# A hybrid decoder step on one core: the projection in two token halves with the mLSTM between its pieces, decode attention alone

## The reference

```python
h = rmsnorm(x, pre_g)
u = h @ w_in                                # 1024 -> 3584 = 28 tiles of 128
qa, ka, va, za, xb, ob, zb = split(u)       # 4 tiles each
a = diff_attention(qa, ka, va)              # 4 heads; sample: 2048 cached keys in 16 pages of 128
a = headwise_rmsnorm(a) * silu(za)
xc = causal_conv(xb); xch = silu(xc)        # 4 taps
qb, kb, vb = xch @ wq, xch @ wk, xb @ wv    # per head, 4 heads of 128
gates = concat(qb, kb, vb) @ w_if + b_if    # input gate, forget gate
hb, C, n, m = mlstm_scan(qb, kb, vb, gates) # running state C (128 x 128 a head)
hb = headwise_rmsnorm(hb * sigmoid(ob)) + skip * xch
y = concat(a, hb * silu(zb)) @ w_out
x = x + rmsnorm(y)
x = x + rmsnorm(sigmoid(x @ ple_gate) * (p @ ple_w))
```

## Time and profile before

| | us |
|---|---|
| median of 3 runs | 1188.6 (1186.11 to 1190.7) |
| profiled execution, its own time | 1184.3 |
| its span, first to last instruction | 1182.6 |
| PE busy | 1007.3 (85%) |
| DVE, ACT, POOL busy | 480.1, 371.6, 72.6 |
| DMA moved | 126.3 MB |

### The profile page before, as it was taken

The page is one execution under the profiler, slowest core; times in us unless marked ns, Lnnn a source line. Parts: engine busy times, 40 slices in busy tenths (PEclk is TensorE's granted clock), DMA queues, the critical chain, the costliest instruction groups (busy, mean ns, idle before and its releaser), DMA issues.

```text
span 1182.6 us, 20550 instructions
## 1 busy us (share of the span) xinstructions
PE 1007.3 (85%) x7424; PEld 829.9 (70%) x7424; DVE 480.1 (41%) x1156; ACT 371.6 (31%) x845; POOL 72.6 (6%) x174
## 2 busy tenths in 40 slices
PE   4899999999995768878887778567788799989997
PEld 4899999999994656556566655344556688667773
DVE  5411010101104845555455455337886534352222
ACT  4322121222212043323323333236665432241111
POOL 2100000000002011001001001001110000000000
PEclk9999999999995689999999999769999899989998
DMA  6111121111103154765665665566000222212220
GB/s 200 41 54 48 43 56 36 54 38 52 54 1 107 35 185 143 226 193 186 210 205 186 207 208 188 171 239 274 2 1 1 76 72 92 73 45 81 81 82 26
DMA packets 88701, 126.32 MB, mean 107 GB/s; under 512 B 8744, under 2 KB 44713, under 8 KB 88636
## 3 DMA queue, kind: packets, MB, share of 16 engines
q1 hardware_dynamic: 88636, 125.44, 32.7%
HBM read 110.00 MB, written 15.41 MB: 106 GB/s over the span
## 4 chain that ended last, share of the span: by engine, by line
PE 65%; DVE 10%; SPq 7%; issue 6%; DMA 5%; ACT 4%; POOL 1%; ACTq 0%; DVEq 0%; POOLq 0%
PE ps L1433 30%; PE ps L1416 9%; PE ps L1417 9%; PE ps L1418 9%; PE ps L1436 8%; SPq L357 4%; SPq L362 3%; DVE pp L1282 3%; DVE pp L1295 2%; DMA Vr<-in_cache_v 2%; DMA Kr<-in_cache_k 1%; DMA Cs<-in_state_C 1%; DMA U<-in_x_prompt 1%; POOL si L561 1%; DVE Caug L1234 1%
## 5 line engine op out<-in xcount | busy, mean ns | idle before, releaser
L1416 PE MATMUL ps<-hhi,whi 128*128 128x352 f32 x672 | 218.6, 325 | 3.5 <-ACT U L588 1.8
L1417 PE MATMUL ps<-hlo,whi 128*128 128x352 f32 x672 | 216.8, 323 | 0.0
L1418 PE MATMUL ps<-hhi,wlo 128*128 128x352 f32 x672 | 216.5, 322 | 0.0
L878 DVE TENSOR_TENSOR wlo<-wst,whi 128x1024 fp32r<-128x1024 f32 x28 | 34.3, 1224 | 255.6 <-ACT whi L583 255.6
L1416 PEld LDWEIGHTS ps<-hhi,whi 128*128 128x128 f32 x672 | 127.2, 189 | 3.8 <-issue 3.8
L1417 PEld LDWEIGHTS ps<-hlo,whi 128*128 128x128 f32 x672 | 127.4, 190 | 0.0
L1418 PEld LDWEIGHTS ps<-hhi,wlo 128*128 128x128 f32 x672 | 127.1, 189 | 0.0
L588 ACT ACTIVATE U<-ps 128x352 f32<-128x352 f32 x84 | 38.7, 465 | 242.8 <-PE ps L1418 241.9
L1436 PE MATMUL ps<-ident,Kr 128*128 128x128 f32 x512 | 69.9, 281 | 37.4 <-DVE kTs L1114 22.0
L1433 PE MATMUL ps<-wh,rh 128*128 128x512 f32 (+1 forms) x288 | 93.2, 405 | 4.6 <-DVE wout_lo L1349 4.6
L1436 PEld LDWEIGHTS ps<-ident,Kr 128*128 128x128 f32 x512 | 58.1, 144 | 51.4 <-issue 37.5
(11 more groups left out here) (293 smaller groups left out, 1507.8 us busy)
## 6 DMA issues: line engine op xcount, KB each, us to landing
Kr<-in_cache_k SPq DMA_DIRECT2D x128, 256.0 KB, 2.7
Vr<-in_cache_v SPq DMA_DIRECT2D x128, 256.0 KB, 3.4
wst<-in_w_in SPq DMA_DIRECT2D x28, 512.0 KB, 3.8
out_y_prompt<-rows SPq DMA_DIRECT2D x16, 512.0 KB, 2.9
U<-in_x_prompt SPq DMA_DIRECT2D x8, 512.0 KB, 3.6
wout<-in_w_out SPq DMA_DIRECT2D x1, 4096.0 KB, 13.9
rows<-in_x_prompt SPq DMA_DIRECT2D x8, 512.0 KB, 4.7
wgate<-in_ple_gate_w SPq DMA_DIRECT2D x1, 4096.0 KB, 25.8
```

The source lines that it names most:

```text
L1416: nc.tensor.matmul(out, hi, hhi[:, k, cols], start=k == 0, stop=False)
L1417: nc.tensor.matmul(out, hi, hlo[:, k, cols], start=False, stop=False)
L1418: last = nc.tensor.matmul(out, lo, hhi[:, k, cols], start=False, stop=k == KC - 1)
```

## The change

What it does:

1. `U` is cut in two, `U0` (tokens 0 to 511 and the 32 sample tokens, 544 columns) and `U1` (tokens 512 to 1023). The order of weight tiles is xb, ob, zb, qa, ka, va, za. For the first half each weight tile is used in two pieces of 272 columns. Then all 28 weight tiles are loaded and split again, for the second half, each in two pieces of 512 columns by 4 of the 8 blocks of the contraction, both into the same bank. That makes 112 pieces.
2. The order of the head tiles is 0, 1, 2, 3, sample, 4, 5, 6, 7.
3. All pieces are stored with Copy. `gate_tiles` applies Sigmoid or Silu later, in place, on four tiles at once, six passes in all, with a load of the function table before and after.
4. The sample mLSTM runs after piece 10, with one to six pieces (`fill`) between its steps. The prompt mLSTM (`chunk(i)`) follows: chunks 0 to 3 between pieces of the first half's end and the second half's begin, chunks 4 to 7 after the conv of the second half. `FILLS` says how many pieces stand between the steps of a chunk. Each half has its own buffers. POOL no longer copies ob into `kbT`; PE transposes it straight from `U`.
5. Decode is alone, nine rounds written out on PE, ACT and DVE. K has a ring of 16 pages (all of a sequence), V of 8. Transposed keys (`kTs`) and scores have two buffers. The values of the previous sequence come in the second half of a round, two groups at a time.
6. SP: `numbers` and `pages` are as before. K of sequence 0 is loaded after the last piece, then 16 stores (states and sample rows) are issued, then the other rounds.

Core of the diff:

```diff
+HALF = SEQ // 2
+FIRST = HALF + SMP
+PIECE = FIRST // 2
+ORDER = [first + n for first in (XB, OB, ZB, QA, KA, VA, ZA) for n in range(4)]
...
+WEIGHTS_DONE = [2 * w + 2 if w < NT else NT + w + 1 for w in range(WEIGHTS)]
...
+FILLS = [(1, 0, 2, 1, 1, 1, 1)] + 3 * [(1, 1, 2, 1, 1, 1, 1)] + [(1, 0, 3, 3, 2, 2, 2), (1, 1, 3, 1, 1, 1, 2),
+                                                               (1, 1, 3, 1, 1, 1, 2), (1, 1, 3, 1, 1, 2, 2)]
```

On SP:

```diff
                 for g in range(GROUPS):
                     k_nums = None if last else numbers(i, g)
                     v_nums = None if first else numbers(i - 1, g)
                     if not last:
-                        if not (first and g < 4):
-                            sp.wait_ge(s["k_used"], i * GROUPS + (g - 3))
-                        pages(ck, Kr, GP * g % 8, k_nums, k_in[g % 4])
+                        if not first:
+                            sp.wait_ge(s["k_used"], i * GROUPS + (g - GROUPS + 1))
+                        pages(ck, Kr, GP * g, k_nums, k_in[g])
                     if not first:
-                        if not (isinstance(i, int) and i == 1 and g < 2):
-                            sp.wait_ge(s["v_used"], (i - 1) * GROUPS + (g - 1))
-                        pages(cv, Vr, GP * g % 4, v_nums, v_in[g % 2])
+                        if not (isinstance(i, int) and i == 1 and g < 4):
+                            sp.wait_ge(s["v_used"], (i - 1) * GROUPS + (g - 3))
+                        pages(cv, Vr, GP * g % 8, v_nums, v_in[g % 4])
...
+            sp.wait_ge(s["piece_done"], EVENTS)
+            stream_pages(0, True, False)
+            sp.wait_ge(s["C_done"], CH)
+            put("out_state", io["C_prompt"][0, 0].rearrange("h d e -> d h e"), Caug[:, :, 0:DH])
...
             stream_pages(1, False, False)
```

On ACT (`fill` stands on each engine, with that engine's share of a piece):

```diff
+            def gate_tiles(tile, hf, fn):
+                U = (U0, U1)[hf]
...
+                nc.scalar.activation(U[:, tile:tile + 4, :], U[:, tile:tile + 4, :], fn).then_inc(s["gated"], 1)
...
+            def fill(n=1):
+                for p in range(filled[0], filled[0] + n):
+                    if p < 2 * NT:
+                        if p:
+                            evict(p - 1)
+                    elif p % 2 == 0:
+                        evict(2 * NT + p // 2 - NT - 1)
+                    if p % 2 == 0 and p // 2 + 1 < WEIGHTS:
+                        split(p // 2 + 1)
...
             act.wait_ge(*done["nT_ready"])
             act.wait_ge(s["cs_in"], 32)
             copy(Cs[:, :, DH], ps[:, 5, 0:SMP], "n_stored")
...
+            fill(4)
```

On PE a chunk goes: projections, `fill(before_turn)`, `finish(i - 1)`, `fill(before_gates)`, gates with the turned k and v and q x k, `fill(before_rows)`, rows and mask products, `fill(before_inter)`, q x state, `fill(before_intra)`, weights x v and the state update, `fill(before_turn_ob)`, ob turned, `fill(after)`. A piece and a decode round are:

```diff
+            def piece(p):
+                w, part = p // 2, p % 2
...
+                pe.wait_ge(s["wlo_ready"], w + 1)
...
+                if e >= 4 and not (p >= 2 * NT and part):
+                    pe.wait_ge(s["u_stored"], e - 3)
...
+                for k in ks:
+                    w_hi, w_lo = whi[:, w % 2, k, :], wlo[:, w % 3, k, :]
+                    mm(out, w_hi, hi[:, k, cols], k == 0, False)
+                    mm(out, w_hi, lo[:, k, cols], False, False)
+                    last = mm(out, w_lo, hi[:, k, cols], False, k == KC - 1)
...
+                def values(g):
+                    pe.wait_ge(v_in[g % 4], 32 * (2 * (i - 1) + g // 4 + 1))
...
+                    last.then_inc(s["v_used"], 1)
...
+                for g in range(GROUPS):
+                    if i < NSEQ:
+                        keys(g)
+                    if g == 1 and i >= 1:
+                        turn_weights()
+                    if i < NSEQ and g >= 1:
                         scores(g - 1)
...
+                    if i >= 1 and g >= 4:
+                        values(2 * g - 8)
+                        values(2 * g - 7)
```

More of the change, by code:

```diff
@@ new lines, in rtok @@
+        def rtok(tile, t0, n):
+            if t0 >= SEQ:
+                return r0[:, tile, HALF + t0 - SEQ:HALF + t0 - SEQ + n]
+            return r0[:, tile, t0:t0 + n] if t0 < HALF else r1[:, tile, t0 - HALF:t0 - HALF + n]
+        rows = [place(f"rows{n}", [P, D], offset=u0_base + VA * FIRST * 4 + n * D * 4) for n in range(2)]
+        rows.append(place("rows2", [P, D], offset=u1_base + VA * HALF * 4))
+        gpost = place("gpost", [P, D], offset=u1_base + VA * HALF * 4 + D * 4)
+        half_k = KC // 2
@@ new lines, in copy @@
+            def copy(out, in_, name, fn=ACT.Copy, **more):
+                nc.scalar.activation(out, in_, fn, **more).then_inc(*(s[name], 1) if name in s else signal[name])
+            for o in range(5):
+                square_x(o)
+                if o >= 1:
+                    store_hi(o - 1)
+                if o == 2:
+                    split(0)
+            for o in range(4, 9):
+                fill()
+                store_hi(o)
+                if o < 8:
+                    square_x(o + 1)
@@ new lines, in _, with fill @@
+            filled = [0]
+            def fill(n=1):
+                for p in range(filled[0], filled[0] + n):
+                    if p % 2 == 0 and p // 2 + 1 < WEIGHTS:
+                        rest(p // 2 + 1)
+                filled[0] += n
+            for o in range(5):
+                scale_x(o)
+                if o >= 1:
+                    store_lo(o - 1)
+                if o == 2:
+                    rest(0)
+            for o in range(4, 9):
+                fill()
+                store_lo(o)
+                if o < 8:
+                    scale_x(o + 1)
@@ L1102, in _, with decode @@
+            for i in range(H):
+                chunk(i)
+            fill()
+            finish(H - 1)
+            fill(3)
+            dve.wait_ge(s["piece_done"], 2 * NT)
+            for h in range(H):
+                conv_second(h)
+                fill(2)
+            for i in range(H, CH):
+                chunk(i)
+            finish(CH - 1)
+            dve.wait_ge(s["u_stored"], EVENTS)
             nc.vector.memset(ps[:, 3, 0:DH], 0.0).then_inc(*signal["den_step"])
-            def stream_dve(i, first, last):
-                G0, t0 = i * GROUPS, i * P
+            def decode(i):
```

1610 lines of the change are left out of this document (862 added, 748 removed).

## The result

The changed kernel is slower: 1291.6 us median of 4 runs (1282.2 to 1293.2) against 1189.5 of the kernel before (now the median of four), ratio 1.085, 95% interval 1.080 to 1.090. The forecast was 1267, its range 1230 to 1297.

A forecast was written before the change was run, and what follows sets the result against it. Decode rounds were taken as bound by SP's instruction stream. Projection end at 493 us, first values 50 later, six rounds of 45 and a last sequence of 43 put prompt attention at 856, +79 us: 1267 us, range 1230 to 1297.

The forecast's parts named there:

- end of the projection stage E: Time by which everything ahead of decode is done: 493 us, bounds 477 and 520, against 421.4 before.
- six rounds: Decode alone: six rounds of P = 45 us each, bounds 39 and 46.5.
- last sequence: End of decode: V alone, softmax some 3 us, transposes, four V groups at 2.2, last combine; 43 us.
- Pieces of 272 columns: First half of the projection: 0.124 us per matmul, bounds 0.123 and 0.159, leaving the projection's 307 us as before.
- the hole: Sample mLSTM: ACT waits for the Cs load ahead of the next weight cast, so PE waits about 9 us.
- Chunks moved under the projection: Prompt mLSTM chunks cost PE 12.6 us each, 100 us for eight, added in full, plus 3 us of waits.
- Decode bound by SP's instructions: Decode rounds: SP's table reads and load issues take 4.8 us a group, 38.4 us for eight groups.
- The handshake: Decode, once a round: V group 4 waits for first values behind K group 4; 6.2 us cold, 4.5 warm.
- Clock: PE in decode: nearly cold rounds of 45 us, clock well under 0.9; at full clock rounds of 43.1.
- DMA or PE is the bound: Rival for decode: SP's issue can run ahead, rounds of 33 us, 1177 us in all; chance 3%.
- No handshake: Rival for decode: SP bound, waits behind V group 4 swallowed, rounds of 39.2 us, 1232 in all; chance 12%.
- Weave stalls: Rival for the projection: late chunk hand-overs or 272-column pieces nearer 0.140; +20 to +32 us, 1293; chance 15%.

The follow-up runs named there:

- the edit: Changed kernel with TensorE doing only the last matmul or transpose of each block in prompt chunks 1 to 7: 1233.9 us, ratio 1.040 to the kernel before.
- experiment 1: Changed kernel with SP issuing K groups two groups ahead of V groups inside a round: 1241.0 us, ratio 1.047 to the kernel before.
- experiment 2: Changed kernel without page table reads, page numbers being the loop's own count: 1190.9 us, ratio 1.003 to the kernel before.
- experiment 7: Changed kernel with V pages read from the table and issued by POOL's queue, K staying on SP: 1157.3 us, ratio 0.975 to the kernel before.
- experiment 10: Experiment 7's kernel with the previous sequence's values spread from the third key group on: 1140.0 us, ratio 0.961 to the kernel before.

## Why the prediction came out

The direction and the mechanism were right; the sum was 25 us low, with every term but one a little too small. Step by step, in the clock of the profiled execution:

| step | forecast | measured |
|---|---|---|
| end of the projection stage E | 493 | 498.6 |
| first values | E + 50 | E + 48.9 |
| six rounds | 270 | 275.0 |
| last sequence | 43 | 50.4 |
| start of the prompt attention | 856 | 872.9 |
| its end to the end of the kernel | as before | +1.5 |
| median over the profiled time | 4.3 | 9.4 |

*Pieces of 272 columns.* A line through the two paces gave 0.124 us. In the trace of after, 25 starts apart:

```profile
61.78 0.28 PE L1582 MATMUL ps<-hlo,whi 128*128 128x272 f32 x1
...
64.92 0.29 PE L1582 MATMUL ps<-hhi,wlo 128*128 128x272 f32 x1
```

that is 0.1256, +2 us over 1224 of them. Another 1.8 us are the restart behind the hole at 71 us, where 18 matmuls ran at 0.228, half the clock (71.03 to 75.2). PE's busy time in the stage is 437.5 us against the 429 that I summed (307 + 100 + 22), and its idle and short waits are 14.1 against 17. Some 5 us of the busy time I can't place. PE was busy 423 of 428.6 us from 70 us on, as forecast; the hole came at 65 to 71 us and not near 60, ended by DVE's `wlo` behind ACT, whose row shows it standing at the states' load:

```profile
66.90 0.23 ACT L701 ACTIVATE Cs<-ps 128x32 f32<-128x32 f32 x1 [7.67 <-DMA Cs<-in_state_C]
```

*Chunks moved under the projection*: 8.3 us measured for the part of a chunk that the edit left out (57.7/7), 8.7 reckoned from the earlier trace rows. "Nearly free in the rounds" was right for work taken away (nothing gained for 61 us) and wrong as a general reading of PE's idle time: work added between the last and first values cost in full (43.6 of 45). The 2.8 us of the earlier trace rows were the sign of it: SP already met PE once a round, at that place.

*Decode bound by SP's instructions*: right, shown by experiments 1, 2 and 7. The floor of 38.6 us a round was measured as 39.4 to 40.0.

*The handshake*: right in place, and in size with some luck. Forecast were 6.2 us for V group 4 when cold (PE at the low clock), 4.5 when warm, and 0 to 1.4 for V group 6; the sum took 6.2 and 0, as if every round were cold. Measured in six rounds: 4.4 to 7.0 us for V group 4, three of them near 4.5, 5.4 in the mean; about 1 us for V group 6 in five of the rounds and 2.2 in one. Together these are the 6.6 us a round, P 45.8 against 45: a first wait taken too long and a second one left out nearly cancelled. The wait comes twice in eight groups, not once.

*Last sequence*: the term that was furthest off. I gave it 43 us and counted its four V groups at 2.2 each. Its V group 4, too, waits for the first values of its own sequence, and these wait for the softmax. In the chain of waits of after that wait stands in the middle:

```profile
850.61 3.43 PE ps L1585 x17
854.06 0.20 ACT pT L701
854.25 0.24 issue
854.50 0.66 PE ps L1582 x16
855.22 0.04 issue
855.32 0.33 SPq L411
```

From the first values of this sequence (854.50) to the start of its last group (866.57) it took 12.1 us, where four times 2.2 are 8.8: the issue and landing of V group 4 come once on top. That is 3.3 of the 7.4 us. The forecast doesn't split its 43 us further, so the rest stays open.

*Clock*: 0.76 over the stage, below the 0.9 that I named. The rows of PE above show both levels: behind the idle 6.72 us the eight transposes took 1.97 us, behind the idle 1.66 us they took 1.09. The rule of the Trainium skill that I had weighed there ("TensorE: Matmul & The Clock Gate", "HAM oscillation — how this bites in real kernels") speaks of DMA waits that are longer than the bursts between them. Behind the 6.72 us the trace agrees; the wait of 1.66 us is shorter than the burst of over 2 us ahead of it, and not every group started cold. PE's busy share was 58%, not under 50, since the records of the same matmuls are longer at the low clock. The 1.47 us that I took for transposes at half clock came from a block that mixes both levels; wholly cold, from their start to that of the scores, they take 1.90 (648.71 to 650.61).

*Runs beside the profile*: the other three runs took 1290.7 to 1293.2, 8 to 11 us more than the profiled one, at a granted clock of 0.903 against its 0.911. Only that one has a trace, so why the term for it was 9.4 us and not 4.3 stays open.

*Rivals*: "DMA or PE is the bound" had the wrong state of the kernel and the right price: freed of the table reads, the round was 33.7 us against the 33 given. "No handshake" is ruled out by the 39.8 us of SP's waits, and its price was right: experiment 1 took them out and gave rounds of 39.4 to 40.0 against its 39.2. "Weave stalls" didn't come: all idle time of PE in the projection stage is 14.1 us, and the pieces of 272 columns ran at 0.1256 and not at 0.140.

## What to carry to other kernels

Count a queue's instructions per round times their distance, as one counts an engine's: if they fill the round, work of other engines beside it is hidden, and moving it to a stage where its engine is the bound costs it in full. A deeper ring gained nothing here while one in-order queue puts the next load of one stream behind the slot of another (no run changed the depth of a ring alone); issue first what others wait for, or give each stream its own queue and slots enough to run ahead. An engine's idle time was slack only outside the stretch in which the binding queue waits for it; what was added inside that stretch counted at once.

## What the runs showed of the hardware

- Reading a page number into a register cost SP more time than issuing the 256 KB load that needs it: 0.66 us from one read to the next against 0.53; leaving the reads out made the changed kernel 100 us faster.
- POOL's queue issued such a group, reads and loads, in 2.31 us, no slower than SP (2.4). From issue to landing a page took 4.8 to 4.9 us on either queue when both ran (DMA 0.98, 345 GB/s), 2.7 (K) and 3.5 (V) when SP issued alone (0.58, a round of the changed kernel).
- Two queues together moved up to 345 GB/s over a round of 27.7 us, 335 in the mean over 160 us (experiment 10). SP alone, with the table reads, gave 214 at most over a round (experiment 1).
